# Order of the weight-product matmuls in two token tiles of a float32 network on one core

## What is computed

```python
h_lat = rms_norm(x, norm_g) * (1.0 + scale) + shift
... = split_cols(h_lat @ w_in)
terms.append(jax.nn.sigmoid(gr) * ((y * jax.nn.silu(zr)) @ w_branch[r]))
x = x + gate * ((terms[0] + terms[1] + terms[2]) @ w_out)
...
v = rms_norm_2(proj[..., A_WIDTH:2 * A_WIDTH], v_gain)   # mixer A
y = u * mixed * jax.nn.silu(z)
return y @ w_out
```

## Time and profile before

| | |
|---|---|
| median of 3 runs | 2580.11 us (2578.04 to 2582.01) |
| profiled execution, span from first to last instruction | 2578.0 us |
| the profiled execution's own time | not given beside its span |
| TensorE matmuls busy | 2502.6 us, 97% |
| VectorE, ScalarE busy | 58%, 48% |
| mean granted TensorE clock | 0.991 |
| read from HBM | 308 MB, 120 GB/s |

### The profile page before, as it was taken

The page is one execution under the profiler, slowest core; times in us unless marked ns, Lnnn a source line. Parts: engine busy times, 40 slices in busy tenths (PEclk is TensorE's granted clock), DMA queues, the critical chain, the costliest instruction groups (busy, mean ns, idle before and its releaser), DMA issues.

```text
span 2578.0 us, 32806 instructions
## 1 busy us (share of the span) xinstructions
PE 2502.6 (97%) x12517; PEld 2015.6 (78%) x12517; DVE 1491.7 (58%) x2454; ACT 1238.1 (48%) x2303; POOL 20.2 (1%) x37
## 2 busy tenths in 40 slices
PE   5999999999999999899999999999999998999999
PEld 2978788677886787788886886878888887888887
DVE  5563333774446444665637666565669946556565
ACT  5652322654245333475426544455456645554643
POOL 1000000000000000000000000000000000000000
PEclk8999999999999999999999999999999999999999
DMA  7412323113320033352531440456555561555554
GB/s 219 125 58 82 115 90 98 42 42 114 90 74 9 17 98 106 98 168 84 178 98 42 140 147 9 147 167 194 163 176 183 172 204 58 182 174 182 179 170 138
DMA packets 163807, 311.54 MB, mean 121 GB/s; under 512 B 10218, under 2 KB 22420, under 8 KB 163396
## 3 DMA queue, kind: packets, MB, share of 16 engines
q1 hardware_dynamic: 161812, 303.75, 37.2%
q0 software_dynamic: 1840, 5.69, 0.9%
HBM read 308.35 MB, written 1.05 MB: 120 GB/s over the span
## 4 chain that ended last, share of the span: by engine, by line
PE 87%; DVE 7%; ACT 3%; issue 2%; DMA 1%; SPq 1%; ACTq 0%; DVEq 0%
PE bank L706 24%; PE bank L708 23%; PE bank L707 23%; PE bank L725 6%; PE bank L810 5%; PE bank L829 4%; DVE neg_max L1823 2%; DVE w_low_part L1453 1%; ACT w_high_part L1006 1%; DMA w_raw<-in_w_mod_dram 1%; PE bank L882 1%; PE bank L936 0%; SPq L558 0%; DVE map_ratio L1836 0%; DVE a_v L1944 0%
## 5 line engine op out<-in xcount | busy, mean ns | idle before, releaser
L1453 DVE TENSOR_TENSOR w_low_part<-w_raw,w_high_part 128x1024 fp32r<-128x1024 f32 (+3 forms) x592 | 695.3, 1190 | 767.4 <-ACT w_high_part L1006 765.8
L1006 ACT ACTIVATE w_high_part<-w_raw 128x1024 fp32r<-128x1024 f32 (+3 forms) x592 | 605.3, 1033 | 883.8 <-PE bank L708 866.9
L706 PE MATMUL bank<-w_high_part,h_high 128*128 128x512 f32 (+3 forms) x2128 | 811.4, 381 | 2.6 <-DVE h_low L1732 1.2
L708 PE MATMUL bank<-w_high_part,h_low 128*128 128x512 f32 (+3 forms) x2128 | 806.6, 379 | 0.0
L707 PE MATMUL bank<-w_low_part,h_high 128*128 128x512 f32 (+3 forms) x2128 | 806.4, 379 | 0.0
L706 PEld LDWEIGHTS bank<-w_high_part,h_high 128*128 128x128 f32 x2128 | 400.4, 188 | 79.6 <-issue 5.1
L708 PEld LDWEIGHTS bank<-w_high_part,h_low 128*128 128x128 f32 x2128 | 400.4, 188 | 74.2
L707 PEld LDWEIGHTS bank<-w_low_part,h_high 128*128 128x128 f32 x2128 | 400.6, 188 | 72.3
L1295 ACT ACTIVATE stage<-bank,neg_max 128x512 f32<-128x512 f32 (+1 forms) x240 | 147.1, 615 | 156.6 <-DVE neg_max L1826 95.5
L725 PEld LDWEIGHTS bank<-ident,stage 128*128 128x128 f32 (+1 forms) x1112 | 124.9, 140 | 115.2 <-issue 98.5
L810 PE MATMUL bank<-k_turned,q_turned 64*128 64x512 f32 (+3 forms) x480 | 185.8, 560 | 2.5 <-ACT stage L1295 1.7
(11 more groups left out here) (246 smaller groups left out, 2194.9 us busy)
## 6 DMA issues: line engine op xcount, KB each, us to landing
w_raw<-in_w_in_dram SPq DMA_DIRECT2D x160, 512.0 KB, 3.4
w_raw<-in_a_w_in_dram SPq DMA_DIRECT2D x96, 512.0 KB, 4.2
w_raw<-in_b_w_in_dram SPq DMA_DIRECT2D x80, 512.0 KB, 4.5
w_raw<-in_w_mod_dram SPq DMA_DIRECT2D x48, 512.0 KB, 3.9
w_raw<-in_w_branch_dram SPq DMA_DIRECT2D x48, 512.0 KB, 4.5
w_raw<-in_a_w_out_dram SPq DMA_DIRECT2D x32, 512.0 KB, 4.6
w_raw<-in_c_w_in_dram SPq DMA_DIRECT2D x32, 512.0 KB, 3.5
w_raw<-in_w_out_dram SPq DMA_DIRECT2D x16, 512.0 KB, 3.9
```

Source lines behind the costliest of these rows:

```text
L706: pe.matmul(o, high, wh, start=(k == 0), stop=False)
L708: mm = pe.matmul(o, low, wh, start=False, stop=(k == u.kt - 1))
L1006: nc.scalar.activation(WH[:, c % PART_SLOTS, 0:kt, 0:width], RAW[:, c % RAW_SLOTS, 0:kt, 0:width], ACT.Copy).then_inc(*S.up("w_high", c))
L1453: v.tensor_tensor(WL[:, s, 0:kt, 0:width], RAW[:, r, 0:kt, 0:width], WH[:, s, 0:kt, 0:width].bitcast(F32), ALU.subtract).then_inc(*S.up("w ...
```

## The change

Inside a chunk the tiles are taken in pairs (2 and 3; or 0 and 1, then 2 and 3). For each k the three products of a pair are issued alternately: `high*wh` of both tiles, `high*wl` of both, `low*wh` of both. At a unit's first chunk both banks of the pair are taken together. What is waited for before a chunk, how the increments are placed on the last matmul of a tile, and the other engines' code stay as they are. The condition products have one tile and keep their order.

```diff
-                    for t in u.tiles:
+                    for pair in (u.tiles[i:i + 2] for i in range(0, len(u.tiles), 2)):
                         if n == 0:
-                            open_banks[t] = take("wide", (u.key, t))
-                        b = open_banks[t]
+                            for t in pair:
+                                open_banks[t] = take("wide", (u.key, t))
                         for kk in range(kt):
                             k = k0 + kk
                             once(left_ready(u.left, k))
...
-                            pe.matmul(o, high, wh, start=(k == 0), stop=False)
-                            pe.matmul(o, high, wl, start=False, stop=False)
-                            mm = pe.matmul(o, low, wh, start=False, stop=(k == u.kt - 1))
...
+                            for t in pair:
+                                pe.matmul(o[t], left[t][0], wh, start=first, stop=False)
+                            for t in pair:
+                                pe.matmul(o[t], left[t][0], wl, start=False, stop=False)
+                            mm = {t: pe.matmul(o[t], left[t][1], wh, start=False, stop=last) for t in pair}
+                        for t in pair:
+                            if n == len(u.chunks) - 1:
+                                mm[t].then_inc(*fills(open_banks[t]))
+                                if t == u.tiles[-1]:
+                                    S.same("w_used", c, f"bank{open_banks[t]}_filled")
+                            elif t == u.tiles[-1]:
+                                mm[t].then_inc(*S.up("w_used", c))
```

More of the change, by code:

```diff
@@ L697, in gemm @@
                             once(left_ready(u.left, k))
-                            high, low = left_high_low(u.left, k, t)
-                            o = banks[b][0:4 if u.left[0] == "cond" else P, 0:width]
                             wh, wl = WH[:, slot, kk, 0:width], WL[:, slot, kk, 0:width]
-                            if low is None:
-                                pe.matmul(o, high, wh, start=(k == 0), stop=False)
-                                mm = pe.matmul(o, high, wl, start=False, stop=(k == u.kt - 1))
-                                continue
@@ L706, in gemm @@
-                            pe.matmul(o, high, wh, start=(k == 0), stop=False)
-                            pe.matmul(o, high, wl, start=False, stop=False)
-                            mm = pe.matmul(o, low, wh, start=False, stop=(k == u.kt - 1))
[L709 to L714, removed]
+                            first, last = k == 0, k == u.kt - 1
@@ new lines, in gemm @@
+                            if u.left[0] == "cond":
+                                o = banks[open_banks[pair[0]]][0:4, 0:width]
+                                both, _ = left_high_low(u.left, k, pair[0])
+                                pe.matmul(o, both, wh, start=first, stop=False)
+                                mm = {pair[0]: pe.matmul(o, both, wl, start=False, stop=last)}
+                                continue
+                            left = {t: left_high_low(u.left, k, t) for t in pair}
@@ new lines, in gemm @@
+                            o = {t: banks[open_banks[t]][:, 0:width] for t in pair}
+                            for t in pair:
[10 more added lines that the diff above has]
+                                mm[t].then_inc(*S.up("w_used", c))
```

## The result

The changed kernel takes 2611.9 us (median of 4 runs, 2610.5 to 2613.1) against 2581.1 us of the kernel before on the same chip: 1.0123 times as long, 95% interval 1.0109 to 1.0137. The forecast was 2603 us with a range of 2590 to 2612. The direction and the main mechanism were right; the loss was 30.9 us and not 22.8, at the very top of the range. The profiled span went from 2578.0 to 2608.5 us, so the traces have 30.5 us to explain.

A forecast was written before the change was run, and what follows sets the result against it. TensorE, with 87% of the chain, was taken to bound the kernel, losing time only at late w_low and at seams between units. Terms summed to 22.8 us on a 2580.1 us median: forecast 2603 us, range 2590 to 2612.

The forecast's parts named there:

- ukv and uq: At these units' starts the second bank is wanted one slot after the first, so TensorE waits: +2.3 us over six seams.
- rival (3): In four-tile units each pair's second bank is late everywhere, 40 seams at 0.4 us: about 2613 us, chance 0.08.
- condition products: Fourth tile's evacuation before these products ends some 0.4 us later, lengthening TensorE's wait for converted weights: +2.4 us over eight seams.
- The slot: Time one 128x512 matmul occupies on TensorE, 0.226 us; claimed unchanged by alternation, a gain of 0.
- rival (1): Repeating the same bank costs 13 ns a matmul, so alternation shortens nearly every one: about 2529 us, chance 0.05.
- b_qk: Twelve units whose weight split queues behind both tiles' evacuation; w_low comes later, 0.90 us a unit: +10.4 us, the largest term.
- a_norm: In two kind-A mixers the chain to the next weight split hangs on the first fill, moving 1.13 us each: +2.3 us.
- Four-tile rope units: TensorE waits for the second bank (0.27 us) and fourth (0.2) at seven seams, more at dq and dk: +4.0 us.
- The covers: For a_z, z, gm, c_x, b_v and branch, short evacuations and banks wanted late hide the change: cost nothing, else 0.4 a seam.
- The gain of 0.5: The next k of the left operand is wanted three slots later, shortening TensorE's waits on L706: -0.5 us.
- VectorE seams and the end: Seven seams evacuated by VectorE, their fills some 0.2 us later, +1.4 us; the last add delayed, +0.5 us.
- (2): No chain hangs on the first fill; engines are held by something else and catch up: 0 to 5 us, 2582, chance 0.07.

The follow-up runs named there:

- middle-chunk run: The change, but only chunks that are neither a unit's first nor its last alternate; 2580.0 us in 11 runs, 1.0001 against the kernel before.
- last-chunk run: The change, but the last chunk of a unit with several chunks goes tile by tile as before; 2590.9 us, 1.0041 against the kernel before.
- late signals: Kernel before in its own matmul order, signal that a pair's first tile is full raised five, three or one slots late: 2597.7 us, 2587.5 us, ratio 1.0003.
- run with the split between the tiles: The change, but in b_qk ScalarE and VectorE split the next chunk's weights between evacuating the two tiles, not after both; 2598.7 us, 1.0070.

## Why the prediction was right in kind and wrong in size

The mechanism was right: time is lost only where something hangs on a bank's fill or on its taking. What failed is the size of terms, above all the moment at which the second bank is wanted, taken as a slot after the first where the code wants both at once (rope 4.0 against 7.6 us, ukv and uq 2.3 against 3.6), and a cover counted at nothing for the narrow units and z (0 against 3.2). That 2611.9 us still lies within the range is luck: its high end came from rival (3) and not from these steps, and condition products priced too high made up for 1.3 us.

**The slot: right.** It stayed 0.226 us with alternation, and the middle-chunk run bounds the effect of the alternation in it at 0.1% of the time. An estimate by the Trainium skill (TensorE: Matmul & The Clock Gate, "Back-to-back issue gap") was 57 us less; no part of that came. Two readings of the rows were off, without harm to the sum. The 1888 of the earlier trace rows are the matmuls with h as left operand; with y (384) and the wide one (224) L706 has 2496 of 128x512, so rival (1) should have stood at 7488 x 13 ns = 97 us less. And of the chain's 87% the page gives 70 to the three lines of weight products, which is not "nearly all".

**b_qk: right mechanism, 10.4 against 11.8.** The chain from ScalarE's first step to w_low was as long as before: 2011.06 - 2001.19 = 9.87 us, against 1988.64 - 1978.76 = 9.88. The step that failed is "10 slots and 0.39 to tile 2 full": after a wait the first matmul occupies 0.34 and not 0.23. That is the 0.11 us between 12.68 and 12.79, and in 12 units it makes 1.3 of the missing 1.4 us. The margin of "some 0.3 us" was read at the matmul, where it had to be read at the load a slot earlier. This did no harm to the sum, as it went by intervals and not by the margin.

**a_norm: right**, 2.0 against 2.3. The chain moved by 1.01 each time and not by 1.13. In the change ScalarE's first copy starts at 1782.29, 16.68 us after that of before, and VectorE's pass over V at 1785.95, only 16.56 after, so 0.12 was made up between the two.

**Condition products: 1.1 against 2.4.** The step "the fourth ends some 0.4 us later" gave 0.17 to 0.26. It was read from the 0.60 us that an evacuation is recorded with, less a slot. But ScalarE's next step starts 0.49 after it (281.99 to 282.48), and 0.49 - 0.23 = 0.26 is the step measured at gm.

**Four-tile rope units: the largest error, 7.6 against 4.0.** The failed step is "it will want the second bank at about 380.76". The code takes both banks of the pair ahead of its first matmul, so the second was wanted at 380.45. With the old numbers the wait is 380.98 + 0.14 (the row above: copy done 385.80, matmul 385.94) - 380.45 = 0.67, not 0.27. The first pair after it takes 0.54 instead of 0.46, but so did the first two matmuls after the transposes before, so that is no new cost. At the fourth bank there is a wait of 0.10 and a restart of 0.08, and 0.07 more is spread over the slots after the two restarts. In all 0.92 at this seam, by the lined-up starts. The steps at the others are 0.75 to 0.92, with 1.04 and 1.40 for dq and dk, which the forecast had set apart. That both evacuations hang on transposes and not on fills was right for seven of the eight, as the last-chunk run left them whole; dq's went with the late fill, as the forecast had said.

**ukv and uq: 3.6 against 2.3**, the same step: "now one slot after, 98.85".

**The covers: partly wrong.** For branch I took "13 slots (2.9 us)" from full to wanted. The unit that follows it is 256 columns wide; its pairs follow at 0.24 us, so 13 of its slots are 1.6 us, little more than half of the cover. VectorE frees the bank at 695.67 + 0.69 = 696.36 and TensorE, which came for it 0.85 us earlier by the profile, starts at 696.51. For z I had named 0.4 a seam if the cover went; it was 0.2, and it went with the early taking of the second bank.

**The gain of 0.5** for the left operand did not show. **VectorE seams and the end: right**, 1.2 and 0.4 against 1.4 and 0.5; another 0.7 us passed between the last add and the end of the span, which no term had and nothing here explains.

**The rivals.** That a slot gets shorter (0.05) and that nothing hangs on the first fill (0.07) are refuted by the middle-chunk run and the late signals. For (2) stood that VectorE's own queue was full at its first step. In the change VectorE waits 1.11 us there for ScalarE (2002.73), so that queue did not hide the late fill. "More is lost in four-tile units", 2613 us at 0.08, named the place where the surplus came from and nearly the time, though not the mechanism: not 40 seams at 0.4 through late fills, but 16 at 0.4 to 1.4, through banks taken early and, after branch, narrow slots. Its chance was too small, since the forecast read the taking of banks from the idea of the change and not from its lines.

## What to carry to other kernels

When a matmul order is changed, write down for each output bank when it is taken and when it is full, from the lines of the code, and see what stands in the other engines' queues behind its evacuation: here the order itself cost nothing, and what it cost came from those two moments. A margin is to be read at the weight load one slot ahead of the matmul, and a cover counted in slots is to be priced with the slots of the unit that gives it. Alternation confined to chunks that neither take nor fill a bank changed nothing that 11 runs could measure.

## What the runs showed of the hardware

Three things I had not expected. A new wait of TensorE costs 0.11 us for its restart in b_qk (0.08 at a rope seam) and gives back the slot in which the load would have run ahead: at 0.23 us late it cost 0.12. The wait column understates a stall (0.70 for 1.02 us). And the granted clock differed between traces in a few stretches in which TensorE pauses, most of all at the end of the hybrid layers. Windows of the kernel before, of the change (some 16 us later for the same work), and of the run with the split between the tiles (columns as the earlier trace rows):

```profile
1685.00:1695.00 10.00, 7.80 (x35) 6.03 (x34) 7.60 (x14) 3.47 (x9) 1.99 (x3) 0.83 0.53 159
...
1715.00:1725.00 10.00, 5.79 (x23) 4.82 (x22) 6.60 (x17) 7.89 (x18) 0.00 (x0) 0.66 0.33 111
```

```profile
1705.00:1715.00 10.00, 8.29 (x40) 6.76 (x41) 6.64 (x13) 4.38 (x7) 1.98 (x3) 1.00 0.64 211
...
1735.00:1745.00 10.00, 8.85 (x36) 7.17 (x37) 6.54 (x16) 6.00 (x15) 0.00 (x0) 0.83 0.19 52
```

```profile
1705.00:1715.00 10.00, 8.12 (x32) 6.48 (x33) 6.53 (x12) 3.43 (x7) 1.99 (x3) 0.83 0.61 203
...
1735.00:1745.00 10.00, 6.64 (x21) 5.30 (x22) 7.02 (x17) 5.99 (x16) 0.00 (x0) 0.69 0.17 54
```

A mean of 0.83 or 0.69 is a part of the window at 1.2 GHz and the rest at 2.4. In the first of its windows the kernel before shows 128x512 matmuls 0.43 us apart, where they are 0.23 apart at full clock:

```profile
1692.24 0.63 PE L708 MATMUL bank<-w_high_part,y_low 128*128 128x512 f32 x1
1692.66 0.63 PE L706 MATMUL bank<-w_high_part,y_high 128*128 128x512 f32 x1
```

In their two windows the three traces lack the clock of (0.17 + 0.34) x 10 = 5.1, of 1.7 and of (0.17 + 0.31) x 10 = 4.8 us. The lined-up starts show what that did. Against the kernel before, the change gains 1.6 and 0.3 us there; against the change, the run with the split between the tiles loses 1.6 and 1.9, which no edit explains. So a difference of 2 to 3 us between two spans can be the clock, and the comparisons above go by lined-up steps and by medians. What decides where it falls was not tried.
